# Two-layer hybrid decoder step: sample states summed by TensorE, last terms loaded in one queue, and a new order at the end of a layer

## What is computed

```python
def step(s, qkv):                       # retention; for the samples one chunk of 8 tokens
    ...
    s_new = s * chunk_decay + jnp.einsum('bhjd,bhje->bhde', kc * k_decay, vc)
    return s_new, o

for e in range(N_EXPERTS):              # experts, two of 16 per token
    act = jax.nn.silu(hf @ w_gate[e]) * (hf @ w_up[e])
    y = y + (act * gates[:, e:e + 1]) @ w_down[e]
return x + y
...
h = rmsnorm(x, norm_g); z = h @ w_in    # next layer's mixer
```

## Time and profile before

| | us |
|---|---|
| median of 3 runs | 847.11 (845.83 to 847.23) |
| the profiled execution, its own time | 848.28 |
| its span | 846.5 |

### The profile page before, as it was taken

How to read it: one execution, slowest core, us unless ns; L and a number is a source line. 1 busy time by engine, 2 the same in 40 slices (tenths; PEclk the granted TensorE clock), 3 DMA queues, 4 the chain that set the end, 5 groups by cost and what they waited for, 6 DMA issues and landing times.

```text
span 846.5 us, 12036 instructions
## 1 busy us (share of the span) xinstructions
PE 822.3 (97%) x4148; PEld 659.8 (78%) x4148; DVE 601.5 (71%) x952; ACT 481.2 (57%) x818; POOL 309.8 (37%) x203
## 2 busy tenths in 40 slices
PE   9999999999999999999899999999999999999994
PEld 6888888888867888887578888889877777888851
DVE  5444564744789999997854464656557899999956
ACT  5533343522478888887353433451235778888863
POOL 0016991300042257732000399621101322267620
PEclk9999999999999999999999999999999999999998
DMA  9832222325938999985952222331396699999839
GB/s 322 264 108 75 76 63 86 89 76 188 408 107 358 403 361 393 395 340 177 318 188 75 74 84 66 84 95 37 99 352 258 207 416 348 382 387 389 303 117 324
DMA packets 68798, 188.19 MB, mean 222 GB/s; under 512 B 10860, under 2 KB 24940, under 8 KB 60538
## 3 DMA queue, kind: packets, MB, share of 16 engines
q1 hardware_dynamic: 54778, 155.50, 51.2%
q0 software_dynamic: 10368, 23.09, 7.8%
q10 hardware_dynamic: 3600, 8.93, 2.9%
HBM read 173.00 MB, written 29.39 MB: 239 GB/s over the span
## 4 chain that ended last, share of the span: by engine, by line
PE 83%; DMA 7%; DVE 6%; ACT 2%; issue 1%; SPq 1%; POOLq 0%; ACTq 0%
PE ps L453 14%; PE ps L457 11%; PE ps L456 11%; PE ps L1374 9%; PE ps L1376 9%; PE ps L1375 9%; PE ps L455 3%; PE ps L1382 3%; DMA wgu<-in_gate_up 2%; DMA back<-y_d 2%; PE ps L1606 2%; PE ps L1546 1%; PE ps L1571 1%; DMA hg<-xn_d,rowidx 1%; DVE gul L2025 1%; DVE x L1823 1%
## 5 line engine op out<-in xcount | busy, mean ns | idle before, releaser
L453 PE MATMUL ps<-wh,hT 128*128 128x512 f32 x475 | 190.9, 402 | 1.6 <-DVE lT L1925 0.9
L2025 DVE TENSOR_TENSOR gul<-wgu,eh 128x1024 fp32r<-128x1024 f32 x128 | 150.7, 1216 | 2.8 <-ACT eh L1074 2.7
L845 POOL DMA_INDIRECT y_d<-y,rowidx x32 | 107.9, 3371 | 117.8 <-DVE y L2050 117.8
L457 PE MATMUL ps<-wh,lT 128*128 128x512 f32 x380 | 148.4, 391 | 0.0
L456 PE MATMUL ps<-wl,hT 128*128 128x512 f32 x380 | 148.2, 390 | 0.0
L1074 ACT ACTIVATE eh<-wgu 128x1024 fp32r<-128x1024 f32 x128 | 129.3, 1057 | 10.3 <-DMA wgu<-in_gate_up 5.8
L2016 DVE SCALAR_TENSOR_TENSOR wl<-raw,gcol,wh 128x512 fp32r<-128x512 f32 x80 | 75.6, 949 | 69.1 <-ACT wh L1047 69.0
L453 PEld LDWEIGHTS ps<-wh,hT 128*128 128x128 f32 x475 | 89.3, 188 | 20.5 <-DVE lT L1925 2.3
L1374 PE MATMUL ps<-eh,hgTh 128*128 128x512 f32 x240 | 96.4, 402 | 0.9 <-issue 0.6
L1376 PE MATMUL ps<-eh,hgTl 128*128 128x512 f32 x240 | 93.8, 391 | 0.0
L1375 PE MATMUL ps<-gul,hgTh 128*128 128x512 f32 x240 | 93.5, 389 | 0.0
(11 more groups left out here) (243 smaller groups left out, 1561.1 us busy)
## 6 DMA issues: line engine op xcount, KB each, us to landing
wgu<-in_gate_up SPq DMA_DIRECT2D x64, 1024.0 KB, 13.3
wdn<-in_w_down SPq DMA_DIRECT2D x64, 512.0 KB, 12.9
raw<-in_w_in SPq DMA_DIRECT2D x79, 256.0 KB, 2.7
raw<-in_w_out SPq DMA_DIRECT2D x32, 256.0 KB, 3.0
back<-y_d SPq DMA_DIRECT2D x14, 512.0 KB, 8.1
s<-in_state_ret POOLq DMA_DIRECT2D x8, 512.0 KB, 5.6
xn_d<-xf ACTq DMA_DIRECT2D x8, 512.0 KB, 5.9
x_in<-in_x_cols SPq DMA_DIRECT2D x8, 288.0 KB, 4.6
```

The source lines that it names most:

```text
L453: pe.matmul(out, both, w_h, start=first, stop=False)
L457: return pe.matmul(out, l[:, t * P:(t + 1) * P], w_h, start=False, stop=final)
L845: pool.indirect_dma_start(out=y_d, out_offset=bass.IndirectOffsetOnAxis(ap=rowidx[:, 1, e:e + 1], axis=0), in_=y[s][:, :], in_offset=None, ...
L2025: ve.tensor_tensor(gu_pair(gul, gul3, e, s, p), gu_pair(wgu, wgu3, e, s, p), gu_split(e, p)[:, :].bitcast(F32), ALU.subtract).then_inc(glo, 1)
```

## The change

1. The new states of heads 0 and 1. TensorE first adds the old state by a product with the identity and then the new product in the same bank; ScalarE evacuates the sum with the decay as its scale (`end_state` on both engines) and VectorE's `sample_state` is gone. The constant that weights the keys is divided by the decay to make up for it.
2. ScalarE's order at the transition: the load of the square-root table and `end_mask(L, 1)` now stand ahead of `w_hi` 0 to 2, then the state of head 0, `w_hi` 3, and the state of head 1. At the end of the last layer the table load is ahead of the mask, and the two evacuations stand behind the diagonals of the gates.
3. `back[1]` is loaded by SP behind `back[0]`.
4. The samples' second terms are written to the rows right behind their first ones, so that one load of 128 rows takes the place of two of 64 at the end of the last layer.
5. TensorE's first tile of layer 1 (`first_tile`): high-part products of blocks 0, 1 and 2 first, the low-part ones behind them. The idle turns are fewer: 0, 11 and 3 for 10, 15 and 6 at the transition, 4 for 16 at the end.
6. VectorE adds tile 0's terms ahead of splitting weight block 3. The last tile's scaling and store are cut in two halves of 512 columns.

```diff
     def kdecay_sample():
-        late = np.where(np.arange(NH) >= LATE, f(DECS), f(0))[None]
-        return np.exp(((DECS - 1.0 - (p % DECS)).astype(f)[:, None] - late) * log_g[None]) * scale
+        return np.exp((-1.0 - (p % DECS)).astype(f)[:, None] * log_g[None]) * scale
...
                 sp.dma_start(back[0][:, :], y_d[0:P, :]).then_inc(row_ld[0], 16)
+                sp.dma_start(back[1][:, :], y_d[TOK:TOK + P, :]).then_inc(second_ld, 16)
                 for u in range(2, 2 * NT):
...
-                    dst = term(LAST, 0)[NSAMP * k:NSAMP * k + NSAMP, :] if t == LAST and L + 1 == NL else back[i][0:n, :]
-                    sp.dma_start(dst, y_d[k * TOK + t * P:k * TOK + t * P + n, :]).then_inc(third_ld if i == 2 else row_ld[t], 16)
+                    if t == LAST and L + 1 == NL:
+                        if k == 0:
+                            sp.dma_start(term(LAST, 0)[:, :], y_d[SEQ:TOK, :]).then_inc(row_ld[LAST], 16)
+                    else:
+                        first_row = SEQ + NSAMP if i == 2 * NT - 1 else k * TOK + t * P
+                        sp.dma_start(back[i][0:n, :], y_d[first_row:first_row + n, :]).then_inc(third_ld if i == 2 else row_ld[t], 16)
...
+            def end_state(L, h):
+
+                sc.wait_ge(skv_mm, 6 * L + 4 + h + 1)
+                for n in range(2):
+                    last = sc.activation(s0_end[h][:, 4 * n:4 * n + 4, :], ps[B_END[h][n]][:, :].rearrange("p (b e) -> p b e", b=4),
+                                         ACT.Copy, scale=float(chunk_decay[1][h]))
+                last.then_inc(s_new, 1)
...
             for L in range(NL):
                 if L:
+                    end_state(L - 1, 0)
                     for s in range(RAW, EARLY[L]):
                         w_hi(L, s)
-                table(ACT.Sqrt)
+                    end_state(L - 1, 1)
                 if L == 0:
+                    table(ACT.Sqrt)
...
                 sc.wait_ge(dpe, 2 * NE * (L + 1))
+                table(ACT.Sqrt)
+                end_mask(L, 1)
                 if L + 1 < NL:
                     for s in range(RAW):
                         w_hi(L + 1, s)
-                end_mask(L, 1)
-                if L + 1 == NL:
-                    table(ACT.Sqrt)
+                else:
                     gate_diagonals()
-                for s in range(3):
-                    sc.wait_ge(y_sc[s], 16 * EUSES[s] * (L + 1))
-                sc.dma_start(back[1][:, :], y_d[TOK:TOK + P, :]).then_inc(second_ld, 16)
+                    for h in range(LATE):
+                        end_state(L, h)
...
+            def first_tile(L):
+
+                def high(s):
+                    S = W_STEPS * L + s
+                    pe.wait_ge(wlo, S + 1)
+                    pe.matmul(ps[0][:, :], hT[:, s, 0:P], wh[S % SPL][:, :], start=(s == 0), stop=False)
+                    pe.matmul(ps[0][:, :], hT[:, s, 0:P], wl[S % SPL][:, :], start=False, stop=False)
+
+                pe.wait_ge(hi_done, mix_hi_done(L) + 1)
+                high(0)
+                high(1)
+                mix_rows(L, 0, (1,))
+                high(2)
+                pe.wait_ge(lo_done, mix_lo_done(L) + 1)
+                for s in range(3):
+                    pe.matmul(ps[0][:, :], lT[:, s, 0:P], wh[(W_STEPS * L + s) % SPL][:, :], start=False, stop=False)
+                mix_rows(L, 1)
+                win_mm(L, 3, 0)
...
                 pe.wait_ge(gain_ld, end_loads(L))
+                for n in range(2):
+                    pe.matmul(ps[B_END[h][n]][:, :], ident, s0_end[h][:, 4 * n:4 * n + 4, :], start=True, stop=False)
                 pe.wait_ge(vb_done, NH * L + NH - LATE + h + 1)
...
-                    for h in range(LATE):
-                        sample_state(L - 1, h)
-                    for s in range(RAW, EARLY[L]):
-                        w_lo(L, s)
                     combine(L - 1, 0, 0)
                     second_row(L - 1, 0)
                     second_row(L - 1, 1)
+                    for s in range(RAW, EARLY[L]):
+                        w_lo(L, s)
                     mix_lo(L, 0, (0,))
```

More of the change, by code:

```diff
@@ L117, in constant_tables @@
     }
+    parts["pair"][0:NSAMP, -1, 0] += NSAMP
+    parts["pair"][0:NSAMP, -1, 1] = LAST + 1
     at, cols, n = {}, [], 0
@@ L123, in constant_tables @@
         cols.append(a)
-    block = np.stack([P * (np.arange(2 * NT) % NT) - NO_ROW, P * np.arange(2 * NT) - NO_ROW], 1)
+    first_row = P * np.arange(2 * NT)
+    first_row[-1] = SEQ + NSAMP
+    block = np.stack([P * (np.arange(2 * NT) % NT) - NO_ROW, first_row - NO_ROW], 1)
     tri = np.concatenate([-1.0 * (p[:, None] >= p[None, :]), np.ones((P, P)), np.tile(np.repeat(p, 2), (P, 1)),
@@ L1315, in _ @@
                 sc.wait_ge(xn_done, NT * NL + i + 1)
-                if t < LAST:
+                if i + 1 == NT:
+                    for half in range(2):
+                        cols = slice(512 * half, 512 * half + 512)
+                        sc.wait_ge(xn_done, NT * NL + i + half + 1)
+                        sc.dma_start(o["y_prompt"][0, t * P:(t + 1) * P, cols], xn[0][t][:, cols]).then_inc(xn_st, 16)
+                elif t < LAST:
                     sc.dma_start(o["y_prompt"][0, t * P:(t + 1) * P, :], xn[0][t][:, :]).then_inc(xn_st, 16)
@@ L1623, in end_state @@
                 pe.wait_ge(gain_ld, end_loads(L))
+                for n in range(2):
+                    pe.matmul(ps[B_END[h][n]][:, :], ident, s0_end[h][:, 4 * n:4 * n + 4, :], start=True, stop=False)
                 pe.wait_ge(vb_done, NH * L + NH - LATE + h + 1)
                 for n in range(2):
-                    last = pe.matmul(ps[B_END[h][n]][:, :], kv_end[0:NSAMP, h, :], vb[h][0:NSAMP, 4 * n:4 * n + 4, :], start=True, stop=True)
+                    last = pe.matmul(ps[B_END[h][n]][:, :], kv_end[0:NSAMP, h, :], vb[h][0:NSAMP, 4 * n:4 * n + 4, :], start=False, stop=True)
                 last.then_inc(skv_mm, 1)
@@ L1641, in _ @@
                     mix_rows(L, 0, (0,))
-                    idle_turns(0, 6)
-                    for t in range(NT):
+                    idle_turns(0, 3)
+                    first_tile(L)
+                    for t in range(1, NT):
                         pe.wait_ge(lo_done, mix_lo_done(L) + 2 * t + 1)
@@ L1646, in _ @@
                             win_mm(L, s, t)
-                            if s == 1 and t == 0:
-                                mix_rows(L, 0, (1,))
-                            if s == (2 if t == 0 else 1) and t + 1 < NT:
+                            if s == 1 and t + 1 < NT:
                                 mix_rows(L, t + 1)
@@ L1794, in _ @@
             pe.wait_ge(s_new, LATE * (NL - 1) + 1)
-            idle_turns(3, 16)
+            idle_turns(3, 4)
             pe.wait_ge(gdiag_done, 4)
@@ L1800, in _ @@
                     idle_turns(3, 12)
-                pe.wait_ge(row_ld[t], 16 + 32 * NL)
+                pe.wait_ge(row_ld[t], 16 + 32 * NL - (16 if t == LAST else 0))
                 ks = 1 if t == LAST else 2
@@ L1904, in later_turns @@
             ve.tensor_copy(pidx[:, :], tmpf[:, :])
[L1905 removed]
+            link(ve.tensor_scalar(small_tab[:, :], tmpf[:, :], float(TOK), float(NSAMP - TOK), ALU.is_ge, ALU.mult))
+            link(ve.tensor_tensor(small_tab[:, :], small_tab[:, :], tmpf[:, :], ALU.add))
+            link(ve.tensor_scalar(tmpf[:, :], tmpf[:, :], float(SEQ + NSAMP), -float(NSAMP), ALU.is_ge, ALU.mult))
             ve.tensor_tensor(tidx[:, :], small_tab[:, :], tmpf[:, :], ALU.add).then_inc(v["a"], 1)
@@ L2006, in last_norm @@
                                                            in1=gain[0:n, cols], op0=ALU.mult, op1=ALU.mult)
-                    else:
+                    elif i + 1 < NT:
                         last = ve.scalar_tensor_tensor(out=xn[0][t][:, :], in0=x[:, t, :], scalar=rstd[:, t:t + 1], in1=gain[:, :],
                                                        op0=ALU.mult, op1=ALU.mult)
+                    else:
+                        for half in range(2):
+                            cols = slice(512 * half, 512 * half + 512)
+                            last = ve.scalar_tensor_tensor(out=xn[0][t][:, cols], in0=x[:, t, cols], scalar=rstd[:, t:t + 1], in1=gain[:, cols],
+                                                           op0=ALU.mult, op1=ALU.mult)
+                            if half == 0:
+                                last.then_inc(xn_done, 1)
                     last.then_inc(xn_done, 1)
@@ L2198, in gated @@
                 ve.tensor_tensor(on[t][:, :, :], on[t][:, :, :], heads(zq(t, "g")), ALU.mult).then_inc(on_done, 1)
-            def sample_state(L, h):
-                ve.wait_ge(skv_mm, 6 * L + 4 + h + 1)
-                for n in range(2):
-                    v = s0_end[h][:, 4 * n:4 * n + 4, :]
-                    last = ve.scalar_tensor_tensor(out=v, in0=v, scalar=float(chunk_decay[1][h]),
```

(4 more changed lines are left out.)

6 lines of the change are left out of this document (2 added, 4 removed).

## The result

| | before | after |
|---|---|---|
| median of 22 runs each, us | 847.14 (845.57 to 850.51) | 849.13 (847.12 to 850.89) |
| ratio, 95% interval | | 1.0021 (1.0014 to 1.0029) |
| the profiled execution, its own time | 848.28 | 848.01 |
| its span | 846.5 | 846.1 |

The change makes the kernel 0.21% slower, 1.8 us. The two spans say the opposite, so they can't be subtracted. I read three lengths instead, with two marks that both kernels have. The **transition** runs from the start of the last evacuation of layer 0's expert output to the start of ScalarE's split of weight block 4. The **end** runs from the start of the same evacuation in layer 1 to the end of the span. The rest lies in between.

The account below looks back on a forecast made before the run. TensorE, busy 97% of the span, was taken as the bound, with term landings pacing the transition. Transition +1.8, end +0.3 and −0.6 sum to +1.5 on the median 847.11: 848.6 us, range 845.2 to 850.4.

Parts of the forecast that it names:

- Step 1: Transition: table load and mask ahead delay ScalarE's split of block 0 by 3.7 us and SP's `back[0]` load by 1.8.
- Step 2: Transition, both tile 0 terms in SP's queue: first lands after 3.7 us, VectorE's first addition starts 0.7 us later.
- step 5: Transition: tile 3's second term stays as late as before, VectorE waits 1.5 to 2 us, transition ends 1.8 us later in all.
- Step 3: Transition: VectorE without `sample_state` gains nothing by itself; the block-3 split moves into an existing hole and costs nothing.
- step 7: End: evacuating head 1's state ahead of tile 0's square costs +0.3 us; storing the last tile in halves gives −0.6.
- Step 4: Transition, TensorE's high-part products first: the second half's transposes come earlier, removing VectorE's 0.23 us wait, −0.2 us.
- Step 6: Transition: TensorE idles about 1.7 us instead of 1.0, and nothing is charged for it.
- (a): Rival, transition: tile 3's late load comes in its turn, so the transition costs 0.0; −0.3, 846.8 us; chance 0.25.
- (b): Rival, the faster side: first load lands after 3.3 us, tile 3 does not wait; −1.7, 845.4 us; chance 0.17.
- (c): Rival, transition: TensorE idles about 3.1 us and its clock falls to half speed; +4.9, 852.0 us; chance 0.12.

Follow-up runs that it names:

- the full rows: Changed kernel, but the last tile's two loads at the transition fetch 128 rows into 128 partitions instead of 64 into 64; ratio to before 1.0025.
- the splits first: Changed kernel, but at the transition ScalarE splits blocks 0 to 2 ahead of the table load and the mask, as before; ratio to before 0.9986.
- the one-queue run: Kernel before with one edit: SP issues `back[1]` right behind `back[0]`, in place of ScalarE; ratio to before 1.0034.
- the best version: Changed kernel with blocks 0 to 2 split first, tile 0 squared ahead of head 1's state, and 128-row loads for the last tile; ratio to before 0.9980.

## Why the prediction was right, step by step

- **Step 1, ScalarE's order: right in mechanism and size.** Predicted were the splits 3.7 us later and `back[0]` 1.8. They started at 404.32 and `back[0]` was issued at 406.30, which is 3.6 and 1.8 later, less the 0.30 by which this execution was late. The drain that the Trainium skill (ScalarE: Activation LUTs, What ACT_TABLE_LOAD costs) states did not come: the load took 1.28 and the next operation followed 0.02 us behind it. Undoing the order gave 3.0 us back (1.0021 to 0.9986); by itself it made the transition 3.0 longer.
- **Step 2, one queue: the first landing right, the second not.** `back[0]` landed after 3.7 us, as forecast. `back[1]` was to land 1.5 us behind it, when the first addition was just done; it landed 2.5 behind it, 5.8 from its issue, and VectorE waited 1.22 us. The sum had no term for this wait, and it did not come out wrong by it, because VectorE then had to wait for tile 3 anyway (step 5). In 410 to 412 the transfers ran at 381 GB/s (360 with the full rows, whose second term was waited for 0.70). They ran at 414 to 416 in the kernels where block 3's load was issued 2.2 us ahead of the terms instead of 0.5, and there nobody waited. With the splits first the second landed 1.3 us behind the first, and so it did at the end of the changed kernel. So "the first gains, the second costs nothing" held only where no other load was just ahead in the queue.
- **Step 3, `sample_state` gone gains nothing: right.** VectorE was idle 2.87 us ahead of the first addition. The block-3 split at its new place ended at 414.57, just ahead of `hT` at 414.60, and cost nothing, as said. What it gave lies at the end: with the old state added by TensorE, TensorE is busy until tile 3's terms are used at 828.00, as step 7 had it, without the 1.36 us of idle time that grew to 2.81 in the one-queue run.
- **Step 4, high parts first: right.** The wait of 0.23 us ahead of the second `lT` is gone.
- **Step 5, tile 3's terms: right in size, the reason open.** They came as late as before, 13.4 us behind their issue, and the transition was 1.94 us longer against 1.8. The wait itself was 0.88 instead of the 1.5 to 2 that the prediction named as its sign: the missed 1.22 of step 2 had used up the rest. Only the later landing counts of two waits in a row, so the error of step 2 was hidden, and that is luck. "For a reason that no row tells" was wrong: a row of the windows would have told, 176 to 180 GB/s at a full DMA share in 417 to 419 of the kernel before, as the full rows then showed.
- **Step 6, TensorE's idle time: 2.69 us instead of 1.7**, by the wait for `back[1]`. No charge was right in the profiled execution. That it is right in the others is not shown.
- **Step 7, the end: +0.3 right, −0.6 wrong.** The square started at 828.34 (828.6 forecast) and tile 0's scaling made VectorE the bound, with no idle time ahead of tile 3's root (833.84). Moving the square ahead returned 0.37. The halves were worth 0.6 by the one landing of the earlier trace rows, and the second was to land after 2.8; it took 3.1. Four landings of the whole store now lie between 2.7 and 3.5, so the term was no larger than their scatter. The end changed by −0.1 instead of −0.3.
- **Sum and base.** +1.5 forecast, +1.85 read in the two stretches, +1.8 by the ratio. The 848.6 stands 0.5 below the 849.1 measured. The bounds that the prediction names for its own range (2.2 for 1.8, 0 or 0.9 for 0.6) give 848.3 to 849.6 and not 847.4 to 849.8; the measured time lies in both. The rivals: (a), the late load in turn, did not come; (b) would have needed the issue by 405.6; (c), the clock, did not come in the change's profiled execution, but it did in four variants. Its condition, "more than the 1.36 us", does not sort them: the clock fell behind 1.09 and stayed behind 2.69.

## What to carry to other kernels

Before you move an operation ahead of another on an in-order engine, follow its product to the queues that wait for it: here a split of weights held a load, and behind this load stood the one that everybody waited for. A load into 64 partitions can take more time than one into 128 with twice the bytes, and the load issued ahead of it can land late by it; look at GB/s beside the DMA share. Ask of each such gain whether the median shows it too: here that of ScalarE's order did, that of the full rows alone did not. Read a small difference by stretches between marks that both traces have, since the spans of two executions differ by more than such a change moves.

## What the runs showed of the hardware

- **64 rows against 128.** While two loads of 256 KB into partitions 0 to 63 ran, the slow microseconds of four kernels show 131 to 193 GB/s with the DMA engines fully busy. With 128 rows each, 512 KB, the rate was 410 to 414 (375 to 410 in the best version), and the last of them landed at 423.5 instead of 425.4.
- **The clock behind idle time.** The granted clock stayed at 1.00 behind 2.69, 2.35 and 2.26 us of TensorE's idle time, and fell to 0.50 behind 1.09, 2.09, 2.50, 2.81 and 3.57. The length of the gap alone does not decide. A fall cost 1.7 us in eight products (5.37 for 3.67) or in eleven turns (4.22 for 2.55).
- **Two loads of one queue.** Issued 0.40 us apart with a block load just ahead, they landed 3.7 and 5.8 us behind their issue. In two queues without one it was 4.7 and 5.0, and 4.8 and 5.0 with the splits first; in one queue without one, 3.6 and 4.5. So one queue brings the first sooner by 1.0 us, and the second is late only behind the block load.
- **Landing of a store.** 512 KB of the last tile took 2.7, 3.2, 3.5 and 3.5 us in four kernels, its halves of 256 KB 3.0 and 3.1 in the changed one. A difference under 0.8 us in one such row carries nothing.
